# Sums of squares of 24 normalised blocks: eight small fp32 matmuls per pair of blocks, or two full-array rounded matmuls per block

## The chip, the cores and the metric

The program runs on one core of a Trainium2 chip. The metric is the time of one execution on the device, in microseconds. The engines are TensorE (PE, with its weight loads PEld), VectorE (DVE), ScalarE (ACT), GpSimd (POOL) and SyncE (SP, which issues the weight DMAs). Each engine runs its own list of instructions in order and waits for the others by semaphores.

## The reference

Two blocks of two layers each run one after the other on x (256 tokens, 1024 channels). The first is a transformer with attention and retention layers; the change does not touch it. The second is a hybrid layer, run twice, with three branches: a convolution, an MLA attention of 8 heads, and a dilated attention of 24 heads of width 64. What matters here is the norm of the dilated queries and keys:

```python
h = rmsnorm(x, norm_g)
proj = h @ w_in
...
dq = rmsnorm(dq.reshape(B, S, DIL_GROUPS, DIL_HEADS, DIL_HEAD_DIM), dil_q_norm_g[:, None, :])
dk = rmsnorm(dk.reshape(B, S, DIL_GROUPS, DIL_HEADS, DIL_HEAD_DIM), dil_k_norm_g[:, None, :])

def rmsnorm(x, g):
    xf = x.astype(jnp.float32)
    y = xf * lax.rsqrt(jnp.mean(xf * xf, axis=-1, keepdims=True) + EPS)
    return (y * g.astype(jnp.float32)).astype(x.dtype)
```

Each head's 64 channels get the reciprocal root of their mean square. With channels on partitions, two heads fill a block of 128 partitions, and the mean goes over 64 partitions.

## The kernel before

Channels lie on partitions and the 256 tokens along the free axis. All dense products use weights in blocks of 128x1024 fp32 (8 tiles of 128x128). SyncE loads a block into one of 4 places of `raw`. ScalarE rounds it (`hi`, L1239, raw to `whi`, of the rounded type fp32r), VectorE forms the rest (`lo`, L1782, raw minus whi into `wlo`). The activations `h` are held in the same two parts. TensorE then makes each product out of three fp32r matmuls: whi by the high part of h (L544), whi by its low part (L545), wlo by the high part (L546). A block of 128 outputs is 8 x 3 matmuls of 256 columns, into one of the 2 places of the PSUM tensor `G`. TensorE may start block j only when the output of block j-2 has been copied out of `G` (`slot_free`).

In each hybrid layer 24 such blocks (H_DQ + j, j = 0 to 23) make the dilated q (12) and k (12). The order is written by hand, per engine, in a loop over j:

- TensorE runs block j. At even j from 2 on it then runs `d_sums(j - 2)` (L1082) for the pair j-2, j-1. These are matmuls in plain fp32 of 64x64 ones (`bones`, two blocks of ones on the diagonal) by the squares in `sq`, four source lines of instructions, two matmuls for each block of the pair. The first block's sums go to `Tp`, the second's, with the halves crossed over, to `O`. Beside this stand the sums of the MLA latent (j = 1, 2), its rotary key (3), its projections (5), and from j = 19 the transposes of the MLA heads into `Tp` (L1078). `Tp` has 2 places, handed out in turn (a `Ring`): a use waits until the use two before it has been read (`t_free`). The loop of the values (H_DV, 12 token blocks) follows, with the last pair and the last three transposes in it.
- ScalarE waits for block j, squares it from `G` into one of 8 places of `sq` (L1639), copies it to `dqk` (L1640), rounds weight block j+4 (L1239), and at even j from 2 on runs `d_root(j - 2)`: three Ln (L1625 to L1627) and one Exp (L1630) over both blocks of the pair into `at`, which has 4 places. `d_root(j)` waits for `d_norm` to have reached j-2, that is for VectorE to have finished tile j-3. At j = 6 stands one square over 3072 columns for the MLA rows (L1652), at j = 9 a small Ln and Exp that need VectorE's reduction of it.
- VectorE forms `wlo` of weight block j+4 (L1782), then from j = 3 on `d_norm_tile(j - 3)` (L2359), which multiplies `dqk` by the gain and by `at`. Between these stand the MLA rows' reduction (j = 8, L2322), scaling (11, L2328), gain (12, L2334) and rotation (14 and 16, L2344 to L2349), whose end (`qk_ready`) TensorE's transposes need.
- GpSimd, after block 7, copies part of `h` to `hy` (L506), which the value blocks from the ninth on need, and makes the first head's `bias` (L512, L519). Otherwise it is idle here.

Of the kernel before, what the change touches and what calls it, by code (L numbers as in the profile page):

```python
# [90 lines left out]
HYB_T = 2 + 1 + 12 + 8 + 8 + 16  # L91
# [106 lines left out]
def build(nc, a, out):  # L198
# [8 lines left out]
    with ctx:  # L207
# [7 lines left out]
        x = sb("x", [P, KT, T])  # L215
        sq = sb("sq", [P, KT, T])
# [111 lines left out]
        wkp = sb("wkp", [P, T], stack=second)  # L328
        second.close()
# [69 lines left out]
        hy_ready = sem("hy_ready")  # L399
        weights_ready = sem("weights_ready")  # L400
# [40 lines left out]

        def crossed(j):

            return O[:, T * (j // 2 % 2):T * (j // 2 % 2) + T]
# [40 lines left out]
        def _(pool):  # L485
# [13 lines left out]
            for l in range(LAYERS2):  # L499
# [3 lines left out]
                pool.wait_ge(blk_done, B_HYB + H_DQ + 7 + l * HYB_BLOCKS)  # L503
# [21 lines left out]
        def _(pe):  # L525
# [451 lines left out]
            for l in range(LAYERS2):  # L977
# [104 lines left out]
                def d_sums(j):  # L1082

                    slot = use_t()
                    pe.wait_ge(d_sq, l * 24 + j + 2)
                    for n in range(2):
                        for r in (0, 64):
                            c = 64 - r if n else r  # L1090
                            to = crossed(j) if n else Tp[:, slot, 0:T]
                            ins = pe.matmul(to[c:c + 64, :], bones[r:r + 64, r:r + 64], sq[r:r + 64, (j + n) % 8, :],  # L1092
                                            start=True, stop=True)
                    ins.then_inc(t_done, 1)

                pe.wait_ge(in_hyb, 64)
                for j in range(24):
# [5 lines left out]
                    if j >= 2 and j % 2 == 0:  # L1103
                        d_sums(j - 2)
# [10 lines left out]
                for j in range(12):  # L1115
                    if j == 8:
                        pe.wait_ge(hy_ready, l + 1)
                    run_tokens(B_HYB + H_DV + j // 4 * 4, G_HYB + H_DV + j // 4 * 4, j % 4, b4, g4,
                               crossed=j >= 8)
                    if j == 0:  # L1120
                        d_sums(22)
                    if j < 3:
                        mla_transposes(5 + j)
# [103 lines left out]
        def _(act):  # L1227
# [316 lines left out]
            for l in range(LAYERS2):  # L1544
# [73 lines left out]
                def d_root(j):  # L1618


                    slot = wait_t()
                    c = j % 4
                    if j >= 4:
                        act.wait_ge(d_norm, l * 24 + j - 2)
                    act.activation(at[:, c, :], Tp[:, slot, 0:T], ACT.Ln, bias=EPS, scale=1.0 / HD)  # L1625
                    act.activation(at[0:64, c + 1, :], crossed(j)[64:128, :], ACT.Ln, bias=EPS, scale=1.0 / HD)
                    act.activation(at[64:128, c + 1, :], crossed(j)[0:64, :], ACT.Ln, bias=EPS,  # L1627
                                   scale=1.0 / HD).then_inc(t_free, 1)
                    act.wait_ge(t_free, L1_T + l * HYB_T + t_ring.n)
                    act.activation(at[:, c:c + 2, :], at[:, c:c + 2, :], ACT.Exp, scale=-0.5).then_inc(d_rs, 1)  # L1630
# [4 lines left out]

                for j in range(24):
                    done(H_DQ + j)
                    dq = gslot(G_HYB + H_DQ + j)
                    act.activation(sq[:, j % 8, :], dq, ACT.Square).then_inc(d_sq, 1)  # L1639
                    freed(act.activation(dqk[:, j, :], dq, ACT.Copy), H_DQ + j)  # L1640
                    next_hi(H_DQ + j)
                    if j >= 2 and j % 2 == 0:
# [30 lines left out]
                for j in range(12):  # L1673
# [7 lines left out]
                    if j == 0:  # L1681
                        d_root(22)
# [87 lines left out]
        def _(dve):  # L1770
# [435 lines left out]
            for l in range(LAYERS2):  # L2206
# [91 lines left out]
                def mla_in():  # L2298
# [12 lines left out]
                    dve.wait_ge(t_free, L1_T + l * HYB_T + 4)  # L2311
# [43 lines left out]
                def d_norm_tile(j):  # L2355
                    dve.wait_ge(d_rs, l * 12 + j // 2 + 1)
                    kind = j % 3
                    gain = nq[:, kind:kind + 1] if j < 12 else lcol[:, L_DK + kind:L_DK + kind + 1]
                    dve.scalar_tensor_tensor(out=dqk[:, j, :], in0=dqk[:, j, :], scalar=gain, in1=at[:, j % 4, :],  # L2359
# [318 lines left out]
```

## Time and profile before

| | |
|---|---|
| time, median of 3 runs | 1438.99 us (1437.01 to 1441.0) |
| profiled execution | 1440.09 us, span 1438.3 us |
| granted TensorE clock | 0.999 of full speed |
| TensorE busy | 1422.2 us, 99% |
| VectorE busy | 1040.6 us, 72% |
| ScalarE busy | 857.1 us, 60% |
| GpSimd busy | 91.9 us, 6% |
| the pairs' matmuls, L1092 | 96 into Tp and 96 into O |

The 24 blocks of dilated q and k begin at about 748 us in the first hybrid layer and at about 1103 us in the second; the last square of theirs stands at 835.4 and 1189.7. A row of the timeline gives start, duration, engine, line, operation, tiles and count. Matmuls overlap, so what one costs is read from start to start, not from its duration. The same holds, to a smaller degree, for ScalarE and VectorE: an instruction may start up to 0.1 us before the record of the one ahead of it ends.

### The profile page before, as it was taken

To read this page: it belongs to the slowest core of one execution; us is meant where nothing else is said; L and a number is where in the kernel's file an instruction comes from. 1 tells how busy PE (TensorE), PEld (TensorE's weight loads), DVE (VectorE), ACT (ScalarE), POOL (GpSimd) and SP (SyncE) were. 2 spreads that over 40 slices of the span, in tenths; PEclk is the share of its full clock that TensorE was granted. 3 is DMA by queue.
4 is the path that set the end of the run, shared out by engine and by line. 5 is a ranking of instruction groups with operands and counts; after the bars stand their busy time and mean duration, and the time that the engine had idled before them with its cause. 6 is when DMAs were issued, how large, how long until landed. Compare 5 with 4: busy or idle time off the path is not lost.

```text
span 1438.3 us, 30495 instructions
## 1 busy us (share of the span) xinstructions
PE 1422.2 (99%) x11812; PEld 1334.3 (93%) x11812; DVE 1040.6 (72%) x1782; ACT 857.1 (60%) x1482; POOL 91.9 (6%) x148
## 2 busy tenths in 40 slices
PE   8999999999999999999999999999999999999999
PEld 6888999999979999999998989899999898989999
DVE  2888899887685677865675857886677585787664
ACT  4566666655556666545566776565566686665553
POOL 0101011110000000000001000220000100031000
PEclk9999999999999999999999999999999999999999
DMA  9976699997664465766663555346666355534663
GB/s 364 337 207 218 238 331 335 341 356 234 204 227 151 151 191 177 234 195 198 192 225 118 173 160 161 116 122 199 193 193 226 105 176 170 153 104 139 188 203 118
DMA packets 81122, 291.93 MB, mean 203 GB/s; under 512 B 9185, under 2 KB 10465, under 8 KB 80882
## 3 DMA queue, kind: packets, MB, share of 16 engines
q1 hardware_dynamic: 68274, 244.31, 52.6%
q0 software_dynamic: 12304, 45.26, 9.4%
q8 instruction: 81, 1.33, 0.4%
q10 hardware_dynamic: 432, 0.79, 0.1%
q14 instruction: 31, 0.25, 0.1%
HBM read 289.27 MB, written 1.05 MB: 202 GB/s over the span
## 4 chain that ended last, share of the span: by engine, by line
PE 91%; DVE 4%; ACT 3%; issue 1%; DMA 0%; SPq 0%; DVEq 0%; ACTq 0%
PE G L544 23%; PE G L546 22%; PE G L545 22%; PE G L603 3%; PE G L605 3%; PE G L604 3%; DVE wlo L1782 2%; PE Tp L997 1%; ACT whi L1239 1%; PE O L1174 1%; PE Tp L1092 1%; PE S L1064 1%; PE S L1140 1%; PE Tp L1078 1%; PE G L625 1%
## 5 line engine op out<-in xcount | busy, mean ns | idle before, releaser
L1782 DVE TENSOR_TENSOR wlo<-raw,whi 128x1024 fp32r<-128x1024 f32 x442 | 541.2, 1228 | 250.9 <-ACT whi L1239 249.3
L1239 ACT ACTIVATE whi<-raw 128x1024 fp32r<-128x1024 f32 x442 | 466.8, 1058 | 207.9 <-PE G L546 153.5
L544 PE MATMUL G<-h,whi 128*128 128x256 f32 x2064 | 581.5, 282 | 0.3 <-DVE wlo L1782 0.2
L545 PE MATMUL G<-h,whi 128*128 128x256 f32 x2064 | 571.2, 277 | 0.0
L546 PE MATMUL G<-h,wlo 128*128 128x256 f32 x2064 | 571.1, 277 | 0.0
L544 PEld LDWEIGHTS G<-h,whi 128*128 128x128 f32 x2064 | 388.0, 188 | 15.7 <-issue 14.5
L545 PEld LDWEIGHTS G<-h,whi 128*128 128x128 f32 x2064 | 387.9, 188 | 0.8 <-issue 0.5
L546 PEld LDWEIGHTS G<-h,wlo 128*128 128x128 f32 x2064 | 387.7, 188 | 0.0
L1790 DVE CUSTOM_DVE_ANT_0 aw<-aw,cs,cols 128x1024 f32<-128x1024 f32 x80 | 101.4, 1278 | 0.0
L544 PE MATMUL G<-ah,whi 128*128 128x256 f32 x352 | 97.2, 276 | 0.0
L545 PE MATMUL G<-ah,whi 128*128 128x256 f32 x352 | 97.2, 276 | 0.0
L546 PE MATMUL G<-ah,wlo 128*128 128x256 f32 x352 | 97.2, 276 | 0.0
L544 PE MATMUL G<-yh,whi 128*128 128x256 f32 x272 | 75.9, 279 | 1.7 <-ACT cF L1570 1.2
L490 POOL DMA_DIRECT2D aw<-in_ada x80 | 42.4, 530 | 544.5 <-DVE mod L1790 510.5
L545 PE MATMUL G<-yh,whi 128*128 128x256 f32 x272 | 75.3, 277 | 0.0
L546 PE MATMUL G<-yh,wlo 128*128 128x256 f32 x272 | 75.3, 277 | 0.0
L603 PE MATMUL G<-whi,h 128*128 128x512 f32 x176 | 70.7, 402 | 0.8 <-ACT rv L1272 0.5
L605 PE MATMUL G<-wlo,h 128*128 128x512 f32 x176 | 69.2, 393 | 0.0
L604 PE MATMUL G<-whi,h 128*128 128x512 f32 x176 | 68.8, 391 | 0.0
L545 PEld LDWEIGHTS G<-ah,whi 128*128 128x128 f32 x352 | 66.1, 188 | 0.0
L546 PEld LDWEIGHTS G<-ah,wlo 128*128 128x128 f32 x352 | 66.1, 188 | 0.0
L544 PEld LDWEIGHTS G<-ah,whi 128*128 128x128 f32 x352 | 66.1, 188 | 0.0
(442 smaller groups left out, 2323.9 us busy)
## 6 DMA issues: line engine op xcount, KB each, us to landing
raw<-in_w SPq DMA_DIRECT2D x444, 512.0 KB, 4.0
aw<-in_ada POOLq DMA_DIRECT2D x80, 512.0 KB, 5.3
adaw<-in_ada SPq DMA_DIRECT2D x8, 1024.0 KB, 15.4
sn<-in_uq POOLq DMA_DIRECT2D x2, 768.0 KB, 5.0
x<-in_x SPq DMA_DIRECT2D x1, 1024.0 KB, 4.9
pt<-in_ukv POOLq DMA_DIRECT2D x2, 512.0 KB, 6.6
out<-x SPq DMA_DIRECT2D x4, 256.0 KB, 2.3
dec<-in_dec ACTq DMA_DIRECT2D x1, 512.0 KB, 7.7
```

Source lines behind the costliest of these rows:

```text
L490: pool.dma_start(aw[:, r % ADA_SLOTS, :], a["ada"][16 + r]).then_inc(ada_raw[r % ADA_SLOTS], 16)
L544: pe.matmul(o, wh, mv[:, 0:T], start=(k == 0), stop=False)
L545: pe.matmul(o, wh, mv[:, T:2 * T], start=False, stop=False)
L546: ins = pe.matmul(o, wl, mv[:, 0:T], start=False, stop=(k == k_of - 1))
L603: pe.matmul(o, hh, wh, start=(k == 0), stop=False)
L604: pe.matmul(o, hl, wh, start=False, stop=False)
L605: ins = pe.matmul(o, hh, wl, start=False, stop=(k == KT - 1))
L625: pe.matmul(o[n], w[:, slot, k * P:(k + 1) * P], src[:, k, 0:T], start=(k == 0 and w is whi), stop=False)
L997: ins = pe.transpose(Tp[:, slot, j * P:(j + 1) * P], src[:, c:c + P], ident[:, :])
L1239: act.activation(whi[:, s, :], raw[:, s, :], ACT.Copy).then_inc(w_hi, 1)
L1782: dve.tensor_tensor(wlo[:, s, :], raw[:, s, :], whi[:, s, :], ALU.subtract).then_inc(w_lo, 1)
L1790: return dve.tensor_tensor_reduce(out=w, in0=w, in1=cs[:, :], scale=1.0, scalar=cols[:, C_ADAB + n:C_ADAB + n + 1], op0=ALU.mult, op1=ALU.add,
```

## The change

The sums are made for each block by itself, with the rounded type. `sums` is a copy of `bones` in fp32r. ScalarE squares block j into one of 2 places of `sq`, and then copies the square, rounded, to `sq_hi` (3 places). GpSimd forms the rest, `sq_lo` = sq minus sq_hi. TensorE runs two 128x128 matmuls of 256 columns, sums by sq_hi and sums by sq_lo, into one place of `Tp`; `O` is no longer used for it. ScalarE then runs one Ln and one Exp of 256 columns a block. `at` is used in 2 places, j % 2, where it was 4, and `d_root(j)` waits for VectorE's tile j-2. `sq_hi` and `sq_lo` lie over the places 2 to 7 of `sq`. GpSimd's copies to `hy` and its first bias now stand behind all 24 subtractions. The load of another activation table moves from the first to the second value block.

```diff
-HYB_T = 2 + 1 + 12 + 8 + 8 + 16
+HYB_T = 2 + 1 + 24 + 8 + 8 + 16
...
+        parts = ExitStack()
+        sb("gap_parts", [P, 2, T], stack=parts)
+        sq_hi = sb("sq_hi", [P, 3, T], f32r, stack=parts)
+        sq_lo = sb("sq_lo", [P, 3, T], f32r, stack=parts)
+        parts.close()
...
+        sums = sb("sums", [P, P], f32r, stack=second)
...
-                pool.wait_ge(blk_done, B_HYB + H_DQ + 7 + l * HYB_BLOCKS)
+                for j in range(24):
+                    pool.wait_ge(d_hi, l * 24 + j + 1)
+                    pool.tensor_tensor(sq_lo[:, j % 3, :], sq[:, j % 2, :], sq_hi[:, j % 3, :], ALU.subtract).then_inc(d_lo, 1)
...
                 def d_sums(j):
                     slot = use_t()
-                    pe.wait_ge(d_sq, l * 24 + j + 2)
-                    for n in range(2):
-                        for r in (0, 64):
-                            c = 64 - r if n else r
-                            to = crossed(j) if n else Tp[:, slot, 0:T]
-                            ins = pe.matmul(to[c:c + 64, :], bones[r:r + 64, r:r + 64], sq[r:r + 64, (j + n) % 8, :],
-                                            start=True, stop=True)
-                    ins.then_inc(t_done, 1)
+                    pe.wait_ge(d_lo, l * 24 + j + 1)
+                    pe.matmul(Tp[:, slot, 0:T], sums[:, :], sq_hi[:, j % 3, :], start=True, stop=False)
+                    pe.matmul(Tp[:, slot, 0:T], sums[:, :], sq_lo[:, j % 3, :], start=False, stop=True).then_inc(t_done, 1)
...
-                    if j >= 2 and j % 2 == 0:
+                    if j >= 2:
                         d_sums(j - 2)
...
                 def d_root(j):
                     slot = wait_t()
-                    c = j % 4
-                    if j >= 4:
-                        act.wait_ge(d_norm, l * 24 + j - 2)
-                    act.activation(at[:, c, :], Tp[:, slot, 0:T], ACT.Ln, bias=EPS, scale=1.0 / HD)
-                    act.activation(at[0:64, c + 1, :], crossed(j)[64:128, :], ACT.Ln, bias=EPS, scale=1.0 / HD)
-                    act.activation(at[64:128, c + 1, :], crossed(j)[0:64, :], ACT.Ln, bias=EPS,
-                                   scale=1.0 / HD).then_inc(t_free, 1)
+                    if j >= 2:
+                        act.wait_ge(d_norm, l * 24 + j - 1)
+                    act.activation(at[:, j % 2, :], Tp[:, slot, 0:T], ACT.Ln, bias=EPS, scale=1.0 / HD).then_inc(t_free, 1)
                     act.wait_ge(t_free, L1_T + l * HYB_T + t_ring.n)
-                    act.activation(at[:, c:c + 2, :], at[:, c:c + 2, :], ACT.Exp, scale=-0.5).then_inc(d_rs, 1)
+                    act.activation(at[:, j % 2, :], at[:, j % 2, :], ACT.Exp, scale=-0.5).then_inc(d_rs, 1)
...
+                if l == 0:
+                    act.wait_ge(in_hyb, 64)
+                    act.activation(sums[:, :], bones[:, :], ACT.Copy)
                 for j in range(24):
                     done(H_DQ + j)
                     dq = gslot(G_HYB + H_DQ + j)
-                    act.activation(sq[:, j % 8, :], dq, ACT.Square).then_inc(d_sq, 1)
+                    if j >= 2:
+                        act.wait_ge(d_lo, l * 24 + j - 1)
+                    act.activation(sq[:, j % 2, :], dq, ACT.Square).then_inc(d_sq, 1)
                     freed(act.activation(dqk[:, j, :], dq, ACT.Copy), H_DQ + j)
+                    act.wait_ge(d_sq, l * 24 + j + 1)
+                    act.activation(sq_hi[:, j % 3, :], sq[:, j % 2, :], ACT.Copy).then_inc(d_hi, 1)
                     next_hi(H_DQ + j)
-                    if j >= 2 and j % 2 == 0:
+                    if j >= 2:
                         d_root(j - 2)
...
                 def d_norm_tile(j):
-                    dve.wait_ge(d_rs, l * 12 + j // 2 + 1)
+                    dve.wait_ge(d_rs, l * 24 + j + 1)
                     kind = j % 3
                     gain = nq[:, kind:kind + 1] if j < 12 else lcol[:, L_DK + kind:L_DK + kind + 1]
-                    dve.scalar_tensor_tensor(out=dqk[:, j, :], in0=dqk[:, j, :], scalar=gain, in1=at[:, j % 4, :],
+                    dve.scalar_tensor_tensor(out=dqk[:, j, :], in0=dqk[:, j, :], scalar=gain, in1=at[:, j % 2, :],
                                              op0=ALU.mult, op1=ALU.mult).then_inc(d_norm, 1)
```

ScalarE's list in the middle of the loop, two iterations of the kernel before (`sq` is the square, `dqk` the copy, `whi` the weight block, the rows with `at` are `d_root`):

```order
L1639 ACTIVATE sq<-G 128x256 [waits blk_done]
L1640 ACTIVATE dqk<-G 128x256
L1239 ACTIVATE whi<-raw 128x1024 [waits blk_done,w_raw2]
L1625 ACTIVATE at<-Tp 128x256 [waits d_norm,t_done]
L1626 ACTIVATE at<-O 64x256
L1627 ACTIVATE at<-O 64x256
L1630 ACTIVATE at<-at 128x512 [waits t_free]
L1639 ACTIVATE sq<-G 128x256 [waits blk_done]
L1640 ACTIVATE dqk<-G 128x256
L1239 ACTIVATE whi<-raw 128x1024 [waits blk_done,w_raw3]
```

The same two iterations of the changed kernel:

```order
L1636 ACTIVATE sq<-G 128x256 [waits d_lo,blk_done]
L1637 ACTIVATE dqk<-G 128x256
L1639 ACTIVATE sq_hi<-sq 128x256 [waits d_sq]
L1237 ACTIVATE whi<-raw 128x1024 [waits blk_done,w_raw2]
L1620 ACTIVATE at<-Tp 128x256 [waits d_norm,t_done]
L1622 ACTIVATE at<-at 128x256 [waits t_free]
L1636 ACTIVATE sq<-G 128x256 [waits d_lo,blk_done]
L1637 ACTIVATE dqk<-G 128x256
L1639 ACTIVATE sq_hi<-sq 128x256 [waits d_sq]
L1237 ACTIVATE whi<-raw 128x1024 [waits blk_done,w_raw3]
L1620 ACTIVATE at<-Tp 128x256 [waits d_norm,t_done]
L1622 ACTIVATE at<-at 128x256 [waits t_free]
```

Every iteration now has a rounding copy ahead of the weight block, and a root with a wait for `d_norm`; before, every second one had a longer root.

TensorE's list behind block 19, at the first transposes of the MLA heads, in the kernel before:

```order
L546 MATMUL G<-h,wlo 128x256
L1078 MATMUL Tp<-ident,qk 96x128 [waits qk_ready,t_free]
L1078 MATMUL Tp<-ident,qk 96x128 x3
L544 MATMUL G<-h,whi 128x256 [waits w_lo,slot_free2]
L545 MATMUL G<-h,whi 128x256
```

The same place in the changed kernel:

```order
L551 MATMUL G<-h,wlo 128x256
L1091 MATMUL Tp<-sq_hi,sums 128x256 [waits d_lo,t_free]
L1092 MATMUL Tp<-sq_lo,sums 128x256
L1083 MATMUL Tp<-ident,qk 96x128 [waits qk_ready,t_free]
L1083 MATMUL Tp<-ident,qk 96x128 x3
L549 MATMUL G<-h,whi 128x256 [waits w_lo,slot_free2]
```

The sums of block 17 now stand between block 19 and the transposes. As each block takes a place of `Tp`, the transposes' `t_free` is now the read of the sums of block 16.

GpSimd's list in a hybrid layer, in the kernel before (`yh` is where `hy` lies):

```order
L502 DMA pt<-in_ukv 128x1024
L506 COPY yh<-h 128x8x64 [waits h_ready,blk_done]
L506 COPY yh<-h 128x8x64 x3
L512 ISA
L512 TENSOR_TENSOR bias<-dist,slopes 128x512 [waits s_free]
```

And in the changed kernel:

```order
L505 DMA pt<-in_ukv 128x1024
L508 ISA
L508 TENSOR_TENSOR sq_lo<-sq,sq_hi 128x256 [waits d_hi] x24
L511 COPY yh<-h 128x8x64 [waits h_ready]
L511 COPY yh<-h 128x8x64 x3
L517 TENSOR_TENSOR bias<-dist,slopes 128x512 [waits s_free]
```

The 24 subtractions have moved in ahead of the copies, which lose their own wait for a block.

## Rows read from the trace of the kernel before

**Rows 1.** The page's first part: busy time, share and instructions of each engine.
```profile
PE 1422.2 (99%) x11812; PEld 1334.3 (93%) x11812; DVE 1040.6 (72%) x1782; ACT 857.1 (60%) x1482; POOL 91.9 (6%) x148
```

**Rows 2.** TensorE's timeline around one pair's sums: start, duration, line, tiles.
```profile
817.00 0.28 PE L546 MATMUL G<-h,wlo 128*128 128x256 f32 x1
...
817.34 0.28 PE L546 MATMUL G<-h,wlo 128*128 128x256 f32 x1
817.54 0.43 PE L1092 MATMUL Tp<-sq,bones 64*64 64x256 f32 x2
...
818.36 0.28 PE L545 MATMUL G<-h,whi 128*128 128x256 f32 x1
```

**Rows 3.** The view of tile bones: count, duration min/median/max in ns, first and last.
```profile
L1092 PE MATMUL Tp<-sq,bones x96: 376/386/427, 757.4 to 1193.1; 64*64 64x256 f32 x96
```

**Rows 4.** TensorE's timeline around the pair at 786 us.
```profile
785.83 0.28 PE L546 MATMUL G<-h,wlo 128*128 128x256 f32 x1
...
787.12 0.28 PE L545 MATMUL G<-h,whi 128*128 128x256 f32 x1
```

**Rows 5.** ScalarE's timeline: the pieces of an iteration.
```profile
738.41 0.42 ACT L1575 ACTIVATE h<-sq 128x256 fp32r<-128x256 f32 x1 [0.17 <-DVE sq L2234]
738.74 0.36 ACT L1570 ACTIVATE cF<-G 128x256 f32<-128x256 f32 x1
...
755.80 0.42 ACT L1611 ACTIVATE cr<-cr 128x256 f32<-128x256 f32 x1
...
805.16 0.38 ACT L1639 ACTIVATE sq<-G 128x256 f32<-128x256 f32 x1 [1.11 <-PE G L546]
...
805.70 1.06 ACT L1239 ACTIVATE whi<-raw 128x1024 fp32r<-128x1024 f32 x1
806.65 0.38 ACT L1625 ACTIVATE at<-Tp 128x256 f32<-128x256 f32 x1
```

**Rows 6.** ScalarE's timeline from the MLA square of iteration 6 to iteration 11.
```profile
783.12 2.77 ACT L1652 ACTIVATE qks<-qk 128x3072 f32<-128x3072 f32 x1
...
787.79 1.08 ACT L1239 ACTIVATE whi<-raw 128x1024 fp32r<-128x1024 f32 x1
...
794.25 0.36 ACT L1639 ACTIVATE sq<-G 128x256 f32<-128x256 f32 x1
...
797.47 0.36 ACT L1639 ACTIVATE sq<-G 128x256 f32<-128x256 f32 x1
```

**Rows 7.** VectorE's busy time in one stretch, count, granted clock, DMA share, GB/s.
```profile
799.10:821.60 22.50, 22.23 (x31) 1.00 0.50 160
```

**Rows 8.** VectorE's timeline beside the blocks, and one row beside a bias product.
```profile
781.53 1.23 DVE L1782 TENSOR_TENSOR wlo<-raw,whi 128x1024 fp32r<-128x1024 f32 x1 [3.37 <-ACT whi L1239]
782.68 0.83 DVE L2359 SCALAR_TENSOR_TENSOR dqk<-dqk,nq,at 128x256 f32<-128x256 f32 x1
...
790.48 3.35 DVE L2322 TENSOR_REDUCE s<-qks 128x32 f32<-128x3072 f32 x1
...
799.08 1.23 DVE L1782 TENSOR_TENSOR wlo<-raw,whi 128x1024 fp32r<-128x1024 f32 x1 [1.59 <-ACT whi L1239]
...
819.65 0.42 DVE L2349 TENSOR_TENSOR qk<-qk,qks 128x256 f32<-128x256 f32 x1
...
821.12 0.48 DVE L2359 SCALAR_TENSOR_TENSOR dqk<-dqk,lcol,at 128x256 f32<-128x256 f32 x1
...
926.51 1.66 DVE L1782 TENSOR_TENSOR wlo<-raw,whi 128x1024 fp32r<-128x1024 f32 x1
```

**Rows 9.** TensorE's timeline at the first transposes of the MLA heads.
```profile
820.98 0.60 PE L1078 MATMUL Tp<-ident,qk 128*96 128x128 f32 x4
```

**Rows 10.** GpSimd's timeline: the copies to hy, and one bias product of 512 columns.
```profile
779.92 3.31 POOL L506 CAST yh<-h 128x512 fp32r<-128x512 f32 x4 [36.12 <-PE G L546]
...
926.05 1.04 POOL L512 TENSOR_TENSOR bias<-dist,slopes 128x512 f32<-128x512 f32 x1 [5.71 <-DVE mn L2403]
```

**Rows 11.** The view of tile bias on GpSimd: duration min/median/max in ns.
```profile
L519 POOL TENSOR_TENSOR bias<-dist,slopes x32: 391/538/1479, 784.4 to 1303.2; 128x128 f32<-128x128 f32 x32
```

More of the change, by code:

```diff
@@ L399, in build @@
         hy_ready = sem("hy_ready")
+        d_hi, d_lo = sem("d_hi"), sem("d_lo")
         weights_ready = sem("weights_ready")
@@ L440, in att_out @@
             return O[:, 0:T] if p < 5 else S[:, p - 5, 0:T]
-        def crossed(j):
-            return O[:, T * (j // 2 % 2):T * (j // 2 % 2) + T]
         def taken(g, r4=0):
@@ L1119, in _ @@
                                crossed=j >= 8)
-                    if j == 0:
-                        d_sums(22)
+                    if j < 2:
+                        d_sums(22 + j)
                     if j < 3:
@@ L1680, in _ @@
                     next_hi(H_DV + j)
-                    if j == 0:
-                        d_root(22)
+                    if j < 2:
+                        d_root(22 + j)
+                    if j == 1:
                         act.preload_act_table_set("exp_and_others")
@@ L2310, in mla_in @@
                         dve.tensor_copy(vm[:, tt, :], S[:, slot, :]).then_inc(s_free, 1)
-                    dve.wait_ge(t_free, L1_T + l * HYB_T + 4)
+                    dve.wait_ge(t_free, L1_T + l * HYB_T + 5)
                     for tt in range(2):
```

## Prediction

> **What bounds the kernel now.** I read the page's busy shares first: TensorE is busy 99% of the span [rows 1], so a change pays only by shortening TensorE's own queue, and costs as soon as it makes that queue wait. Then I went to the timeline of TensorE where the 24 blocks of dilated q and k are computed. A dense block is 24 matmuls that start 0.113 us apart (three from 817.00 to 817.34), 2.72 us in all. Behind every second block stand the eight small matmuls of the sums. The reader should measure them from the last dense start to the second next one: 817.34 to 818.36 is 1.02 us, where two dense steps take 0.23, so one pair of sums costs 0.79 us [rows 2]. The view of the tile `bones` counts 96 such matmuls into Tp, 4 a pair: 24 pairs, 12 a layer [rows 3]. Last I read the neighbours with the least slack: ScalarE and VectorE beside these blocks, and the first transposes of the MLA heads.
>
> **TensorE alone.** Per layer 12 pairs x 0.79 = 9.5 us go, and 24 x 2 matmuls come. They are 128x128 weights by 256 columns of the rounded type, the form of the dense ones, so I take 0.113 us each: 5.4 us. I also take off the 0.3 us for which the pair at 786 stood late behind ScalarE's 2.77 us square (785.83 to 787.12 is 1.29 us where 1.02 is the rule) [rows 4, 6], since the new sums of block 6 are ready before that square. Net 4.3 us a layer, 8.7 us in all. If the two matmuls cost an fp32 form's time instead, up to the 0.79 of a pair, the change would lose 9.5 us a layer; the nearest row is the dense one with the same type and shape, so I take that, and give the other end little.
>
> **ScalarE.** An iteration is: square and copy, 0.54 us to the next start (805.16 to 805.70); the new rounding copy, 0.33 by the nearest row (the 0.42 us copy at 738.41, whose successor starts at 738.74); the weight block's rounding, 0.95 (805.70 to 806.65); one Ln, 0.40; one Exp, at most 0.42, some 0.32 to the next start [rows 5]. Together 2.55 us, at most 2.65, against TensorE's 2.72 + 0.23 = 2.95. The wait on its own square costs nothing: the copy of `dqk` stands between. So ScalarE alone doesn't bind, but has only 0.3 to 0.4 us a block to catch up a delay.
>
> **What is late next: VectorE.** Three places decide it. (a) The new `d_root(j)` keeps its result in 2 places of `at` where the old one used 4, and waits for `d_norm` of tile j-2. That is VectorE's iteration j+1, just one ahead of ScalarE's j+2. (b) VectorE has no idle time to speak of from 799.08 to 821.60 (22.23 us busy of 22.50 [rows 7]): the scaling, gain and rotation of the MLA rows stand there between the weight blocks. Until now nobody looked at this lag. (c) The first MLA transposes on TensorE (820.98) need the end of this row of work (819.65 + 0.42 = 820.07), a slack of 0.9 us, and their Tp slot, which the new ring gives them only when `d_root(16)` has read it [rows 8, 9].
>
> Carried forward from rows: the two pairs before block 6 (1.58) become four singles (0.91), so block 6 ends 0.6 us earlier, and ScalarE's 2.77 us square with it. The reduction on VectorE (790.48) stays where it is, because the weight block ahead of it (787.79) does: ScalarE has the added rounding copies by then. So the square at 794.25 stays too. From there iteration 10 takes 2.55 instead of 3.22 (794.25 to 797.47), the rounding copy ahead of the next weight block gives back 0.33, and VectorE's row starts at about 798.75 instead of 799.08 [rows 6, 8]. Tile 14 (821.12 + 0.48 = 821.60) is then ready at 821.3, the Ln of 0.40 follows, and the transposes start at 821.7: 0.7 us later than the 820.98 of before. By TensorE alone they would have started 3.3 us earlier (9 pairs and the 0.3 less 18 singles). On the way this shows as waits at blocks 12, 16 and 17 and at the sums of 14, since `G` has two places and Tp two slots. Behind the transposes 3 pairs (2.4) become 6 singles (1.4): 1.0 back. Sum without more: -0.3 us a layer.
>
> **GpSimd's share.** It gets one 128x256 subtraction a block. By the rows of `bias`, 1.04 us for 512 columns and 0.39 for 128 at the least, I estimate 0.61 us (0.39 and a third of the difference) [rows 10, 11]. The result is not needed for some 3 us, so its length hides. Its reads don't: where a GpSimd operation is under way, VectorE's next one is stretched. The weight block at 926.51 took 1.66 us instead of 1.23 (0.43 more) beside the bias product of 926.05, and the one at 782.68 took 0.83 instead of 0.48 beside the copies that began at 779.92 [rows 8, 10]. In VectorE's gapless row from 798.75 on every such delay moves the transposes. About 7 subtractions fall into those 22.5 us (one a block of 3 to 3.3 us): 7 x 0.43 = 3.0 us. Bounds: 0 if they slip in without delay, 7 x 0.61 = 4.3 if each holds VectorE for its whole length.
>
> The Trainium skill, SBUF — State Buffer, section on the engine ports, says that the port pair VectorE and GpSimd share is an exclusive lock, held for the whole instruction, and that an operation with two SBUF inputs takes it. The two stretched rows agree in kind: 0.43 is about what was left of the bias product when VectorE's turn came. By that rule every collision in a gapless row costs the length of the subtraction rather than a part of it, which is the third rival below.
>
> **Sum.** Per layer -0.3 + 3.0 = +2.7, for two +5.4 us. The profiled execution took 1440.09 us (span 1438.3 and 1.8 around it), so it would be 1445.5; it lies 1.1 over the median of the runs, 1438.99, so I predict 1444.4 us.
>
> **The rivals.**
> 1. VectorE's row doesn't bind and the gain of TensorE comes whole: 1440.09 - 8.7 - 1.1 = 1430.3 us. For it: TensorE is 99% busy. Against it: the slack of 0.9 us at the transposes and the start of the row at most 0.3 earlier cap what can be gained ahead of them at 1.2 us a layer, with 1.0 behind them 2.2, or 4.4 in all: 1434.6. It would need the row to start earlier than the waits let it. Chance 0.05; 1434 to 1437 for the cap reached in part, 0.05.
> 2. The row binds but GpSimd's reads don't delay it: 2 x -0.3 = -0.6, so 1438.4 us, no change. For it: the weight block at 781.53 kept its 1.23 us beside those copies. Against it: the two stretched rows. Chance 0.25.
> 3. Each subtraction holds VectorE for its whole length: -0.3 + 4.3 = +4.0 a layer, 1447.0 us. Or ScalarE's rounding copy is dearer than 0.33 (0.42 adds 0.1 to each of some 12 iterations in which ScalarE is late), another 1 us a layer, 1449. This decides from the point at which the delay of the row passes 3 us. Chance 0.15.
> My forecast, slower by about 5 us, has 0.50; its own range is 1441.5 to 1449.
>
> A measurement of this kernel can tell 0.3% (4.3 us, so 1434.7 to 1443.3) from no change. Faster takes rival 1 (0.05) and a part of its cap, 0.07 together. Same takes rival 2 (0.25), the rest of the cap, and the lower part of the forecast (0.05): 0.33. Slower takes the rest: 0.60. The range for 8 in 10 runs from 1436.5, which takes in rival 2, to 1450.
>
> **What would show it.** In the new profile: the two matmuls of a block start 0.113 us apart, and the next dense one 0.113 behind (else the first step is wrong). VectorE idles nowhere between about 798.5 and 823. Its weight blocks or `dqk` products there have durations 0.3 to 0.6 us over 1.23 and 0.48, about 7 of them. ScalarE's Ln of d_root 11, 12 and 14 waits for VectorE's `dqk`, 1 to 3 us each. TensorE has gaps of 2 to 5 us a layer before blocks 12 to 19, and the first transposes start 3 to 4 us later than 820.98, counted in the same layer. I am wrong if those Ln wait for nothing, if TensorE's gaps stay under 1 us, or if GpSimd's subtractions take over 2 us and TensorE waits for them itself.

## The result, and the profile after

| | before | after |
|---|---|---|
| time, median of 6 runs | 1439.28 us (1436.77 to 1441.0) | 1446.01 us (1444.59 to 1448.01) |
| ratio of the times | | 1.005, interval 1.0038 to 1.0061 |
| profiled execution, span | 1438.3 us | 1446.2 us |

The change makes the kernel 6.7 us slower; 5.4 us were forecast. The first part of the profile's page, against [rows 1]:

```profile
PE 1422.7 (98%) x11716; PEld 1344.1 (93%) x11716; DVE 1051.2 (73%) x1782; ACT 864.8 (60%) x1531; POOL 140.6 (10%) x196
```

TensorE has 96 instructions fewer and is not less busy. Its waits in the first layer's blocks (745 to 870 us; line waited at, releaser, total us, times, longest) name who holds it up now:

```profile
PE Tp L1083 <- ACT at L1620: 2.0, 1, 2.0
PE Tp L1091 <- ACT at L1620: 1.4, 1, 1.4
PE G L549 <- ACT dqk L1637: 1.0, 2, 0.5
```

L1083 are the transposes, L1091 is the first matmul of the sums, L1620 the Ln of `d_root`. ScalarE's timeline at that Ln shows in brackets what it waited for itself:

```profile
806.32 0.39 ACT L1620 ACTIVATE at<-Tp 128x256 f32<-128x256 f32 x1 [2.74 <-DVE dqk L2359]
...
811.73 0.38 ACT L1620 ACTIVATE at<-Tp 128x256 f32<-128x256 f32 x1 [2.77 <-DVE dqk L2359]
...
818.09 0.39 ACT L1620 ACTIVATE at<-Tp 128x256 f32<-128x256 f32 x1 [1.20 <-DVE dqk L2359]
...
824.30 0.38 ACT L1620 ACTIVATE at<-Tp 128x256 f32<-128x256 f32 x1 [1.06 <-DVE dqk L2359]
```

These are the Ln of `d_root` 11, 12, 14 and 16. So ScalarE's wait is VectorE's lateness handed on. VectorE's scaling of the MLA rows in the kernel before:

```profile
800.82 3.36 DVE L2328 TENSOR_TENSOR qk<-qk,s 128x3072 f32<-128x3072 f32 x1
```

VectorE's timeline in the changed kernel, against [rows 7, 8]; these are the rows longer than their kind (wlo 1.23, scaling 3.36, rotation 0.42, dqk 0.48 in the kernel before):

```profile
800.32 3.84 DVE L2328 TENSOR_TENSOR qk<-qk,s 128x3072 f32<-128x3072 f32 x1
804.19 1.64 DVE L1782 TENSOR_TENSOR wlo<-raw,whi 128x1024 fp32r<-128x1024 f32 x1
...
809.60 1.64 DVE L1782 TENSOR_TENSOR wlo<-raw,whi 128x1024 fp32r<-128x1024 f32 x1
...
813.88 0.85 DVE L2346 TENSOR_TENSOR qk<-qk,lcs 128x256 f32<-128x256 f32 x1
...
817.03 0.96 DVE L2359 SCALAR_TENSOR_TENSOR dqk<-dqk,lcol,at 128x256 f32<-128x256 f32 x1
...
820.23 0.85 DVE L2346 TENSOR_TENSOR qk<-qk,lcs 128x256 f32<-128x256 f32 x1
...
823.26 0.94 DVE L2359 SCALAR_TENSOR_TENSOR dqk<-dqk,lcol,at 128x256 f32<-128x256 f32 x1
```

Seven rows, 0.41 to 0.48 us over each: 3.1 us. Beside them GpSimd's subtractions:

```profile
800.20 0.75 POOL L508 TENSOR_TENSOR sq_lo<-sq,sq_hi 128x256 fp32r<-128x256 f32 x1 [1.79 <-ACT sq_hi L1639]
802.72 2.04 POOL L508 TENSOR_TENSOR sq_lo<-sq,sq_hi 128x256 fp32r<-128x256 f32 x1 [1.77 <-ACT sq_hi L1639]
808.09 2.07 POOL L508 TENSOR_TENSOR sq_lo<-sq,sq_hi 128x256 fp32r<-128x256 f32 x1 [3.34 <-ACT sq_hi L1639]
```

The second one starts under VectorE's scaling (800.32 to 804.16) and ends 0.6 us behind it, while the weight block at 804.19 is stretched; the third stands in the same way under the gains (806.15 to 809.56). So by these rows each holds the other: first GpSimd waits for the operation that VectorE has begun, then VectorE for GpSimd. The Trainium skill, SBUF — State Buffer, section "Who interferes with whom", says that the two engines share one pair of ports under an exclusive lock, and that the one that comes second blocks fully. The rows agree in kind: GpSimd's subtraction is up to 1.3 us longer than its usual 0.74. In size VectorE loses less than such a lock would take: behind the scaling the subtraction has 0.60 us left (804.16 to 804.76), and the weight block is 0.41 us longer.

The end of the chain on TensorE, against [rows 9]:

```profile
824.74 0.64 PE L1083 MATMUL Tp<-ident,qk 128*96 128x128 f32 x4 [1.99 <-ACT at L1620]
825.14 0.37 PE L549 MATMUL G<-h,whi 128*128 128x256 f32 x1
825.34 0.28 PE L550 MATMUL G<-h,whi 128*128 128x256 f32 x1
...
826.16 0.41 PE L549 MATMUL G<-h,whi 128*128 128x256 f32 x1
826.37 0.41 PE L550 MATMUL G<-h,whi 128*128 128x256 f32 x1
826.59 0.41 PE L551 MATMUL G<-h,wlo 128*128 128x256 f32 x1
```

The transposes start 3.76 us later than before (824.74 against 820.98). In the second layer they start 9.02 us later, of which 5.20 lie ahead of that layer's first square, so that layer itself adds 3.8. Just behind them the dense matmuls of the first layer stand 0.21 us apart. The windows there (busy us of PE, PEld, DVE, ACT, POOL with counts, granted clock, DMA share, GB/s) show the clock:

```profile
825.00:826.00 1.00, 1.00 (x10) 1.00 (x9) 0.74 (x2) 1.00 (x5) 0.00 (x0) 0.82 0.80 291
826.00:829.00 3.00, 3.00 (x16) 3.00 (x16) 1.62 (x2) 2.10 (x4) 0.73 (x1) 0.50 0.72 239
829.00:830.00 1.00, 1.00 (x10) 1.00 (x10) 0.00 (x0) 0.23 (x1) 0.00 (x0) 0.98 0.64 70
```

The granted clock fell to 0.50, the 1.2 GHz level, for about 3 us, after TensorE had stood idle 0.49, 1.40, 0.49 and 1.99 us within the last 17.5. Sixteen matmuls at 0.21 instead of 0.113 are 1.5 us. All six executions of the changed kernel have a mean granted clock of 0.995 or 0.996, where the profiled one of the kernel before has 0.999. In the second layer the same three first idle times were enough (0.49 at 1167.34, then these two), and the slow stretch lies ahead of the transposes:

```profile
1171.76 0.39 PE L1091 MATMUL Tp<-sq_hi,sums 128*128 128x256 f32 x1 [1.42 <-ACT at L1620]
1172.75 0.39 PE L549 MATMUL G<-h,whi 128*128 128x256 f32 x1 [0.49 <-ACT dqk L1637]
...
1174.02 0.41 PE L549 MATMUL G<-h,whi 128*128 128x256 f32 x1
1174.23 0.41 PE L550 MATMUL G<-h,whi 128*128 128x256 f32 x1
```

There it costs nothing more, since TensorE would have waited for VectorE anyway: at the transposes only 0.59 us of waiting are left, where the first layer has 1.99.

Last, the step that I had taken for certain. TensorE's timeline around two sets of sums with one block between:

```profile
797.65 0.28 PE L1091 MATMUL Tp<-sq_hi,sums 128*128 128x256 f32 x1
797.76 0.28 PE L1092 MATMUL Tp<-sq_lo,sums 128*128 128x256 f32 x1
797.88 0.28 PE L549 MATMUL G<-h,whi 128*128 128x256 f32 x1
...
800.59 0.28 PE L551 MATMUL G<-h,wlo 128*128 128x256 f32 x1
800.71 0.28 PE L1091 MATMUL Tp<-sq_hi,sums 128*128 128x256 f32 x1
```

From 797.65 to 800.71 are 26 matmuls in 3.06 us: 0.1177 each, not 0.113. The kernel before, from the second matmul of the block behind one pair to that behind the next:

```profile
799.62 0.28 PE L545 MATMUL G<-h,whi 128*128 128x256 f32 x1
...
805.86 0.28 PE L545 MATMUL G<-h,whi 128*128 128x256 f32 x1
```

Two blocks and a pair take 6.24 us there and 2 x 3.06 = 6.12 now. By itself TensorE gains 0.12 us a pair, 1.4 a layer, where I had 4.3 (4.0 without the stall).

### The profile page after: what moved, and what is told of

Read it like the earlier page. It is cut to its first block, busy times and chain, and to the rows that moved or that the text cites. A ratio compares the mean times of both kernels' runs of the same rounds, so it can differ in the third digit from the quotient of the medians.

```text
span 1446.2 us, 30490 instructions
## 1 busy us (share of the span) xinstructions
PE 1422.7 (98%) x11716; PEld 1344.1 (93%) x11716; DVE 1051.2 (73%) x1782; ACT 864.8 (60%) x1531; POOL 140.6 (10%) x196
## 4 chain that ended last, share of the span: by engine, by line
PE 84%; DVE 8%; ACT 4%; issue 2%; DMA 2%; SPq 0%; DVEq 0%; ACTq 0%
PE G L549 21%; PE G L551 20%; PE G L550 20%; DVE wlo L1782 3%; PE G L608 2%; PE G L610 2%; PE G L609 2%; ACT whi L1237 2%; PE Tp L1002 1%; PE O L1172 1%; DMA raw<-in_w 1%; PE S L1069 1%; PE S L1138 1%; DMA adaw<-in_ada 1%; DVE aw L1790 1%
```

## The experiments

Ratios and their intervals are against runs of the kernel before on the same chip. Where no ratio is given, there was one execution, used for its trace.

**Four places of `at`, and no subtraction.** Three kernels: a_at4 has the first edit, a_nopool the second, a_nopool_at4 both. The second edit leaves the rest of the square out of the sums; TensorE's work stays the same.

```diff
-                    if j >= 2:
-                        act.wait_ge(d_norm, l * 24 + j - 1)
-                    act.activation(at[:, j % 2, :], Tp[:, slot, 0:T], ACT.Ln, ...
+                    if j >= 4:
+                        act.wait_ge(d_norm, l * 24 + j - 3)
+                    act.activation(at[:, j % 4, :], Tp[:, slot, 0:T], ACT.Ln, ...
```

```diff
-                    pool.tensor_tensor(sq_lo[:, j % 3, :], sq[:, j % 2, :], sq_hi[:, j % 3, :], ALU.subtract).then_inc(d_lo, 1)
...
-                    pe.matmul(Tp[:, slot, 0:T], sums[:, :], sq_lo[:, j % 3, :], start=False, stop=True).then_inc(t_done, 1)
+                    pe.matmul(Tp[:, slot, 0:T], sums[:, :], sq_hi[:, j % 3, :], start=False, stop=True).then_inc(t_done, 1)
```

Expected of a_at4: 

> The changed kernel with `at` in 4 places again: d_root(j) waits for VectorE's tile j-4 instead of j-2. Theory (VectorE's gapless row, stretched by GpSimd, is late; ScalarE's wait for it is only one of the ways by which it reaches TensorE): ScalarE's waits for dqk L2359 (7.8 and 6.6 us a layer) go, TensorE's wait at the sums of block 14 (1.4) goes, but blocks around 17 then wait for VectorE's wlo and the first transposes still for the rotation's end. Gain 1 to 1.7 us a layer, about 1443.5 us. Rival (the two places of `at` are the whole cause): all waits of TensorE in this stretch go, 3 to 4 us a layer come back, and the time is at or below 1438.

Expected of a_nopool: 

> The changed kernel without GpSimd's 24 subtractions a layer; TensorE's second matmul reads sq_hi again, so its work is the same and the rest sq_lo is left out of the sums. Theory (each subtraction stretches VectorE by 0.45 us): VectorE's wlo and dqk rows are all back at 1.23 and 0.48 between 798 and 822, tile 14 is ready 3.1 us earlier, the first transposes stand near 821.5, and the two layers lose about 0.2 to 0.5 us against the kernel before instead of 4: about 1439 to 1440. Rival (the stretched rows are hidden, and the two matmuls or the wait for d_lo cost the time): under 1 us of change, 1445 or more.

Expected of a_nopool_at4: 

> Both: no subtractions (the rest is left out of the sums, the second matmul reads sq_hi again) and 4 places of `at`. Theory: VectorE's row still has to end before the first transposes, so only part of TensorE's own gain of 3.5 to 4.3 us a layer comes: 1.5 to 2 us a layer, about 1435.5 us. Rival (TensorE's gain comes whole once both waits are gone): 1431 to 1432.

| | median us | ratio to before | interval |
|---|---|---|---|
| a_at4 | 1443.98 | 1.0026 | 1.0008 to 1.0044 |
| a_nopool | 1439.43 | 0.9993 | 0.9971 to 1.0015 |
| a_nopool_at4 | 1435.03 | 0.9953 | 0.9936 to 0.9971 |

Against the 1446.01 us of the changed kernel, 6.6 us are back without the subtractions, 2.0 with more room in `at` alone, 11.0 with both. In a_nopool's trace every row of VectorE between 798 and 822 us has its own length again (scaling 3.36, weight blocks 1.22 or 1.23, `dqk` 0.48), though the loads from memory go on as before. The transposes stand 3.12 us earlier than the 824.74 of the changed kernel, just the 3.1 by which the seven rows were stretched:

```profile
821.62 0.64 PE L1081 MATMUL Tp<-ident,qk 128*96 128x128 f32 x4 [0.32 <-ACT at L1618]
```

Not all of the 6.6 us is GpSimd's hold on VectorE, though. With shorter waits the clock doesn't fall either (granted 1.00 from 745 to 870 us), and from the first layer's first transposes to its last there are 22.61 us instead of 24.19. In a_nopool ScalarE still waits 4.6 us for `dqk` in the first layer; the two places of `at` cost then too. With both edits the transposes stand at 818.31, and what they wait for is VectorE's rotation itself, 0.2 us:

```profile
818.31 0.40 PE L1081 MATMUL Tp<-ident,qk 128*96 128x128 f32 x2 [0.20 <-DVE qk L2347]
```

In a_at4 the same transposes wait 1.37 us for it at 820.32, and a block waits 1.7 us for its `wlo`, so in the first layer four places only move the wait from the Ln to VectorE. In the second layer a block waits 1.7 us for `wlo` and the transposes 2.0 us for the Ln. This trace is of the fastest of the twelve executions of a_at4 (1440.84 us).

**VectorE's row spread out.** a_spread halves the scaling (at j = 11 and 13) and the gain (15, 17), puts the rotations at 19 and 22, and all eight transposes of a layer into the value blocks 0 to 7; with four places of `at`.

```diff
-                    if j == 12:
+                    if j == 13:
+                        mla_part(1)
+                    if j == 15:
...
-                        mla_gain()
-                    if j in (14, 16):
-                        mla_rope(j // 2 - 7)
+                        mla_gain(0)
+                    if j == 17:
+                        mla_gain(1)
+                    if j in (19, 22):
+                        mla_rope((j - 19) // 3)
```

> The changed kernel, subtractions and all, with 4 places of `at`, with the eight MLA transposes moved into value blocks 0 to 7, and with VectorE's MLA work spread: the scaling in halves at j = 11 and 13, the gains at 15 and 17, the rotations at 19 and 22. Theory (the loss comes only from the deadline of VectorE's row): TensorE has no gap over 0.5 us between blocks 8 and 23, ScalarE doesn't wait for VectorE, and TensorE's gain comes nearly whole, 3 to 4 us a layer: about 1432 us. Rival (the doubled collisions or ScalarE's own load of 2.55 of 2.95 us bind anyway): 1437 or more.

Measured: 1444.8 us, ratio 1.0028 (1.001 to 1.0046). That expectation was wrong. The blocks did get faster (ScalarE's square of block 6 to that of 23: 52.35 us, where the kernel before has 55.47), but the second rotation had now come beside GpSimd's copies to `hy`. VectorE's and TensorE's timelines:

```profile
832.88 0.96 DVE L2342 TENSOR_TENSOR qks<-qk,lcs 128x256 f32<-128x256 f32 x1
833.76 0.82 DVE L2343 TENSOR_TENSOR qks<-qk,lcs 128x256 f32<-128x256 f32 x1
...
836.76 1.26 DVE L2347 TENSOR_TENSOR qk<-qk,qks 128x256 f32<-128x256 f32 x1
```
```profile
838.16 0.50 PE L1083 MATMUL Tp<-ident,qk 128*96 128x128 f32 x3 [3.37 <-DVE qk L2347]
```

Six operations of 0.42 took 0.71 to 1.26, and the wait had moved to the new place of the transposes. The clock suffers here too: ten of the twelve executions have a mean granted clock of 0.996 or less.

**Spread, second try, with its control.** a_spread2 puts the transposes two value blocks later and the copies to `hy` behind the eighth subtraction, away from the rotation. b_spread2 is the kernel before, with its fp32 pairs, and the same spreading. a_spread2_nopool has no subtractions and leaves the rest of the square out. a_dve2 has them on VectorE:

```diff
+                    dve.wait_ge(d_hi, l * 24 + j + 1)
+                    dve.tensor_tensor(sq_lo[:, j % 3, :], sq[:, j % 2, :], sq_hi[:, j % 3, :], ALU.subtract).then_inc(d_lo, 1)
                     next_lo(H_DQ + j)
```

Expected of a_spread2: 

> The changed kernel with four places of at (d_root waits for VectorE's tile j-4), VectorE's MLA scaling, gain and rotation halved and spread over its iterations 11 to 22, all eight MLA transposes of a layer in the value blocks 2 to 9, and GpSimd's four copies to hy moved behind the subtraction of tile 7. Theory (VectorE's deadline at the first transposes is what swallows TensorE's gain, and a_spread only moved that deadline to a place where the hy copies stretch the last rotation): the second rotation ends before its transposes are due, TensorE waits for VectorE under 1 us a layer behind block 19, no stretch of lowered clock there; 3.1 us a layer from the blocks and some 2 more from the earlier start of the rest: 1431 to 1434. Rival (GpSimd's reads and ScalarE's added copies cost TensorE as much wherever VectorE's work stands): 1437 or more.

Expected of b_spread2: 

> Control: the kernel before, its fp32 pairs kept, with the same spreading of VectorE's scaling, gain and rotation and the eight MLA transposes in the value blocks 2 to 9. Theory (TensorE's gain in a_spread2 comes from the sums, the spreading only makes room for it): TensorE hardly waits before or after, so 1437.5 to 1440.5, no change. Rival (spreading or the transposes' new place is itself the gain): as fast as a_spread2, 1431 to 1434.

Expected of a_spread2_nopool: 

> a_spread2 without the subtractions on GpSimd: the second matmul of a block reads sq_hi again, so the rest of the square is left out of the sums; the hy copies wait for the eighth rounding copy. Theory (with VectorE's row spread its delays no longer reach TensorE): within 1.5 us of a_spread2, 1431 to 1433. Rival (GpSimd's reads still cost 3 us a layer): 4 to 6 us faster than a_spread2.

Expected of a_dve2: 

> a_spread2 with the subtraction made by VectorE itself, ahead of each wlo, instead of by GpSimd; nothing is left out. VectorE does 24 more operations a layer (0.4 us each by its 256-column products) but is held by none of GpSimd's (0.43 each). Theory: about as fast as a_spread2, 1431 to 1435. Rival (VectorE's spread row has no room for 0.4 us a block, or wlo waits for the rounding copy): 1437 or more.

| | median us | ratio to before | interval |
|---|---|---|---|
| a_spread2 | 1436.03 | 0.9989 | 0.9971 to 1.0007 |
| b_spread2 | 1438.83 | 0.9997 | 0.9984 to 1.001 |
| a_spread2_nopool | 1437.58 | 0.9991 | 0.9979 to 1.0002 |
| a_dve2 | 1437.96 | 0.9987 | 0.9975 to 0.9998 |

In a_spread2 TensorE waits 0.2 us beside the blocks of the first layer and 0.4 in the second; this row is in both:

```profile
PE Tp L1092 <- POOL sq_lo L508: 0.2, 1, 0.2
```

So the waits are gone, and leaving the subtractions out makes nothing faster: where VectorE's row has slack, GpSimd's reads cost nothing that these runs can tell (a_spread2_nopool has waits of its own for `dqk`, 0.9 and 1.2 us). The control says that the spreading is no gain by itself. VectorE can make the subtractions too, but a_dve2 isn't at the 1431 to 1435 expected: in its trace TensorE waits 1.4 us a layer, 1.2 of them for `sq_lo`. Yet a_spread2 itself is only 3.3 us below the kernel before by the medians (1439.31 in these runs), not at 1431 to 1434, and its interval reaches 1: all three numbers that started from a gain of 3 us a layer failed. With no wait left to blame I measured the step between the dense matmuls, as shown above, and found 0.1174 to 0.1178 in nearly every block that follows a set of sums directly, and as a rule 0.113 to 0.115 behind a break.

**What sets the slow step.** a_probe starts from a_spread2. First layer: a tiny fp32 matmul behind the sums. Second layer: the sums in the other order.

```diff
+                    if l == 0:
+                        ins = pe.matmul(Tp[0:64, slot, T:T + 8], bones[0:64, 0:64], bones[0:64, 0:8], start=True, stop=True)
```

> a_spread2 with a third, tiny matmul behind the sums in the first layer (fp32, 64x64 ones by 8 columns, into a part of Tp that nobody reads), and the sums in the other order (sq_lo first) in the second. Theory (the slow step of 0.1177 us is entered at two rounded sums and ended by a break): with the fp32 matmul between, the blocks of the first layer run 0.1133 to 0.114 apart and the block with its sums takes about 3.05 to 3.1 us by what the break costs; in the second layer the order changes nothing, 0.1177. Rival (the slow step belongs to the load on the other engines or on the memory beside these blocks): both layers stay at 0.1177.

The first layer's timeline:

```profile
782.38 0.28 PE L1093 MATMUL Tp<-sq_hi,sums 128*128 128x256 f32 x1
782.49 0.28 PE L1094 MATMUL Tp<-sq_lo,sums 128*128 128x256 f32 x1
782.70 0.28 PE L1096 MATMUL Tp<-bones 64*64 64x8 f32 x2
782.91 0.39 PE L550 MATMUL G<-h,whi 128*128 128x256 f32 x1
783.13 0.28 PE L551 MATMUL G<-h,whi 128*128 128x256 f32 x1
...
785.64 0.28 PE L552 MATMUL G<-h,wlo 128*128 128x256 f32 x1
785.76 0.28 PE L1093 MATMUL Tp<-sq_hi,sums 128*128 128x256 f32 x1
```

From 783.13 to 785.76 are 23 steps of 0.114; this holds for every block behind such a matmul (from 776 us on, 22 steps each, means 0.1141 to 0.1145). In the second layer, without it and with the sums in the other order, the blocks that follow sums directly stay at 0.1178. That speaks against the load on memory or on the other engines as the cause; a_count below, with both steps in turn under one load, excludes it. The break is dear, though: block and sums take 3.38 us instead of 3.06, since the three starts at the change of type lie 0.21, 0.21 and 0.22 us apart (782.49 to 783.13). The 3.05 to 3.1 I had expected was wrong, and the one execution took 1442.45 us.

a_mid puts the sums inside the block, ahead of the fifth (second layer: second) of its eight weight tiles, from block 6 on.

```diff
-                        block1(H_DQ + j)
-                    if j >= 2:
-                        d_sums(j - 2)
+                        run(B_HYB + H_DQ + j, G_HYB + H_DQ + j, 1, 8, of_h, b4=b4, g4=g4,
+                            each_k=lambda k: d_sums(early) if early is not None and k == (4 if l == 0 else 1) else None)
```

> a_spread2 with the two sums matmuls put inside block j instead of behind it (from block 6 on): ahead of the fifth of its eight weight tiles in the first layer, ahead of the second in the second layer. In a_spread2 every block that directly follows the sums has its 24 matmuls 0.1177 us apart, and every block that follows a break of 0.2 us or more 0.1133 to 0.114 apart; that is 0.1 us a block and 4 to 5 us over the two layers, and would be where the missing part of TensorE's gain went. Theory (the slow step is entered at the sums and kept until the next break): the matmuls behind the sums stay 0.1177 apart over the end of the block into the next, so all blocks but the first after a break are slow, as in a_spread2. Rival (the boundary of blocks, with its waits, keeps or enters it): the step falls back to 0.1133 behind the sums or at the next block.

Measured in one execution: 1441.41 us. From 795 us on all stretches between sums in the first layer, each with a boundary of blocks in it, run at 0.1178: the boundary plays no part. Two stretches of the first layer run at 0.1139 and 0.1135. They are those behind sums that came with a break (0.23 us inside the sums at 787.40, a wait of 1.7 us for `sq_lo` at the next), and the sums that then come without one, at 795.40, turn the step to 0.1178. So sums without a break set it; behind a break it mostly goes (in the second layer one of the two such stretches is at 0.1178). At the boundary of blocks the sums wait less: here TensorE waits 1.7 us for `sq_lo` in the first layer, and 1.6 for it and 0.9 for an Ln in the second.

a_count has one sums matmul a block in the first layer, three in the second.

```diff
+                    ins = pe.matmul(Tp[:, slot, 0:T], sums[:, :], sq_hi[:, j % 3, :], start=True, stop=(l == 0))
+                    if l == 1:
+                        pe.matmul(Tp[:, slot, 0:T], sums[:, :], sq_lo[:, j % 3, :], start=False, stop=True)
+                        ins = pe.matmul(Tp[:, slot, T:2 * T], sums[:, :], sq_lo[:, j % 3, :], start=True, stop=True)
```

> a_spread2 with another number of sums matmuls behind a block: one in the first layer (only sums by sq_hi; the rest of the square is left out there), three in the second (a second product by sq_lo, into a part of Tp that nobody reads). Theory (any rounded matmul onto another place of PSUM, put between two dense blocks without a break, sets the slow step): 0.1177 us in both layers. Rival (the number of matmuls between, odd or even, decides): 0.1133 to 0.114 in both layers.

Its timeline in the first layer, only the sums:

```profile
800.62 0.28 PE L1092 MATMUL Tp<-sq_hi,sums 128*128 128x256 f32 x1
...
803.49 0.28 PE L1092 MATMUL Tp<-sq_hi,sums 128*128 128x256 f32 x1
...
806.43 0.28 PE L1092 MATMUL Tp<-sq_hi,sums 128*128 128x256 f32 x1
...
809.30 0.28 PE L1092 MATMUL Tp<-sq_hi,sums 128*128 128x256 f32 x1
```

2.87, 2.94, 2.87 us for 25 matmuls: a fast block and a slow one in turn. With three it alternates too (0.1178 and 0.1135). The one execution took 1436.87 us. Neither expectation was right: with an odd number the sums undo the slow step as often as they set it, with two they leave it behind them in all the blocks seen but one. Why, these runs don't show.

**The same kernel once more.**

> a_spread2 once more, unchanged, since four of its twelve runs stood 6 us above the other eight. By its trace TensorE waits 0.4 us in all beside these blocks and a block with its sums takes 3.06 us where half a pair of blocks took 3.12: 24 x 0.06 x 2 = 3 us less than the kernel before, 1436 us, ratio 0.998. If the upper group of runs belongs to the kernel, a third of the runs lie at 1442 to 1445 again; if not, nearly all lie at 1434 to 1437.

Measured: 1435.57 us (12 runs), ratio 0.9975, interval 0.996 to 0.9991; two of the twelve lie at 1442, the rest at 1433.4 to 1437.8. So in both series this version's median is 3.2 to 3.3 us below that of the kernel before, about a quarter of a per cent; only the second series puts it clear of the noise, and it is some 10 us below the changed kernel. Its profiled execution was one of the upper two (1442.12 us; the other profile of this kernel 1433.92). The windows of 580 to 720 us, far ahead of the change, of a_spread2 and of a_spread2_again:

```profile
580.00:720.00 140.00, 140.00 (x1238) 140.00 (x1237) 91.81 (x121) 72.51 (x105) 0.62 (x2) 1.00 0.66 202
```
```profile
580.00:720.00 140.00, 140.00 (x1192) 140.00 (x1191) 88.86 (x117) 70.26 (x101) 1.06 (x2) 1.00 0.63 195
```

TensorE is busy throughout and has the full clock in both, but does 46 matmuls fewer in the second: 0.1131 against 0.1174 us each, 5.4 us in this window alone. The whole stream of 1393 matmuls around it takes 157.76 us in one (from 564.44) and 163.95 in the other (from 565.82). The first squares of the dilated blocks come at 749.31 and 757.10. So this upper run is the same slow step, caught by chance in a long stretch without breaks. The other upper runs, and executions of the kernel before that stood at 1445 to 1447, were not profiled; that they are the same is likely, not shown.

## Why the prediction was right

1. **TensorE alone, -4.3 us a layer: mis-sized.** The two new matmuls cost what was said, one step each, but the step of all 24 dense ones behind them went from 0.113 to 0.1177, so by itself TensorE gains 1.4. It hardly mattered for the time, because VectorE bound ahead of the transposes either way; that is why a forecast with so wrong a term could stand. It is what a_spread2 then lacked. The stall at 786 went, as forecast.
2. **ScalarE doesn't bind alone: right.** The rounding copies start 0.31 us apart from what follows (0.33 taken), and ScalarE's late Ln wait for VectorE, four in the first layer for 7.8 us in all. TensorE's waits came at blocks 16 and 17 and at the sums of 14, as forecast; ahead of block 12 only 0.3 us are lost (794.40 to 794.82).
3. **VectorE's gapless row: right.** It starts at 798.58 (798.75 forecast) and has no gap; tile 14 is ready at 824.20 (824.3 forecast); transposes 3.76 and 3.8 us late (3.7 forecast). a_nopool_at4, whose transposes wait for the rotation itself at 818.31, shows that the row is the limit, and a_spread2 that nothing binds once it has room.
4. **GpSimd's share, 3.0 us a layer: right.** Seven stretched rows, 3.1 us, and in a_nopool the first layer's transposes are 3.12 us earlier. That the whole kernel was 6.6 us faster there, where 6.0 were forecast, is in part another thing, the clock that no longer fell. Each subtraction takes 0.74 us, not the 0.61 estimated, but the delay it causes was taken from rows of the same collision and held. Rival 3, a delay of the subtraction's whole length, would be 7 x 0.74 = 5.2 us; 3.1 were measured.
5. **Behind the transposes 1.0 us back: too much.** In the second layer 0.54 (first to last transposes 22.59 us, 23.13 before). Two of these blocks run at the slow step, which is 0.2 us; and a pair that stands next to transposes cost only 0.72 us before (1178.38 to 1179.77 with it, 0.67 without it), not the 0.79 taken, which is another 0.2. In the first layer 1.06 us were lost instead: 0.5 back and 1.5 for the lowered clock, which was not foreseen.

So per layer +3.8 - 0.5 = +3.3, in the first another 1.5. With 0.4 us that the stretch between the layers is later, the start of the second layer's squares stands 5.20 behind; the last transposes 8.48 behind; the span is 7.9 longer in these two executions and the median of the runs 6.7. The forecast's 5.4 was short by the clock and by the smaller return. How much of the 1.2 us between 7.9 and 6.7 is the slow step, which falls by chance in long streams, isn't known.

## What to carry to other kernels

Work taken off the busiest engine is worth only what the next deadline lets through: look for a gapless row on a neighbour, and count what each added helper operation does to it, even one on an engine that is 6% busy. A new wait is cheap to widen (four places for two), but the gain moves to the next limit each time, so spread the row and the helper together and run the same spreading without the change as a control. And measure the step between back-to-back matmuls before and after: 4% of it, under a busy share of 99% and a full clock, cost here two thirds of what the change should have saved TensorE (2.6 of 4.0 us a layer).

## What was not expected of the hardware

- A stream of 128x128x256 rounded matmuls without a break has two steps, 0.1133 and 0.1177 us, at a granted clock of 1.00. Which one holds is set where the stream starts or is crossed by other matmuls, and with one exception it then stays, for up to 1487 matmuls at the fast one (175.97 to 344.38) and 1393 at the slow one (565.82 to 729.77 in a_spread2_again). A set of two sums matmuls into another PSUM tensor without a wait leaves the slow one behind it, in some 290 blocks of ten traces; the exception is one block of a_nopool_at4, at 1161.35, that falls back to the fast step after four matmuls. One or three alternate. Behind an idle of 0.2 us or an fp32 matmul the fast one holds as a rule, not always: in the changed kernel the block behind the second transposes (830.36 on) has 0.1177. The slow step is not the change's own either: the kernel before has it, too, in a block behind the MLA's projections (776.99 on) and in longer streams (508.30 to 541.98).
- A tiny fp32 matmul (64x8) between rounded ones costs 0.4 us: from the last sums to the second dense matmul there are 0.64 us (782.49 to 783.13), where two steps take 0.23.
- The clock fell to 0.50 for 3 us behind idle times of 0.49, 1.42 and 0.49 us in a 6 us stretch (second layer); behind nearly the same three in the first layer it stayed at 1.00, and fell only behind a fourth of 1.99. In the profiled execution of a_at4, with idle times of 1.71 and 1.37 eleven us apart, it stayed at 1.00; other executions of that kernel have a mean clock down to 0.995.
